# Sampled tokens' attention: eight PSUM banks dealt out as 3, 2 and 3 in place of 2, 2 and 4

## The reference: what is computed

```python
kc = compress(past_rows(pool_k_cmp), pos_k, w_k)      # 255 compressed keys per sequence
vc = compress(past_rows(pool_v_cmp), pos_v, w_v)
p_c = masked_softmax(einsum(qg, kc)); o_c = einsum(p_c, vc)
idx = top_k(block_score(p_c), 16)                     # 16 blocks of 64 tokens
o_s = softmax(q . k_slc over the chosen blocks) @ v_slc
o_w = softmax(q . 512-token window) @ v_win
o   = gate0 * o_c + gate1 * o_s + gate2 * o_w
```

## Time and profile before

| What | Value |
|---|---|
| median of 3 runs | 2275.66 us |
| the profiled execution, its own time | 2269.16 us |
| its span in the profile | 2267.4 us |
| the stage of the sampled tokens in that span | from about 1472 to 1734 us |
| a step of the first loop (8 of them) | 14.14 us |
| a step of the second loop (7 with keys to turn) | 12.98 us, two of them 1.4 us longer |
| TensorE busy over the span | 91% |
| DMA engines' busy share, first and second loop | 0.82 to 0.86, 0.81 to 0.98 |

### The profile page before, as it was taken

The page is one execution under the profiler, slowest core; times in us unless marked ns, Lnnn a source line. Parts: engine busy times, 40 slices in busy tenths (PEclk is TensorE's granted clock), DMA queues, the critical chain, the costliest instruction groups (busy, mean ns, idle before and its releaser), DMA issues. The chain is left out here.

```text
span 2267.4 us, 37830 instructions
## 1 busy us (share of the span) xinstructions
PE 2070.7 (91%) x16137; PEld 1393.5 (61%) x16137; DVE 868.8 (38%) x2212; ACT 581.1 (26%) x1481; POOL 132.4 (6%) x144
## 2 busy tenths in 40 slices
PE   8898989898989898599999999589878999999998
PEld 5565657575756565456777777455666666666543
DVE  3545364545454545301666666434321000010112
ACT  2323232323232223000445444233351000000000
POOL 1001010101000000000000000022120000000000
PEclk9999999999999999799999999799997999999999
DMA  4101010101020100402000000398695111110011
GB/s 134 38 11 49 11 49 12 48 11 48 14 54 19 41 21 2 148 19 68 20 10 11 11 10 1 92 321 298 246 348 173 42 33 32 32 48 17 0 65 60
DMA packets 121585, 151.22 MB, mean 67 GB/s; under 512 B 27866, under 2 KB 105090, under 8 KB 112866
## 3 DMA queue, kind: packets, MB, share of 16 engines
q1 hardware_dynamic: 110724, 76.78, 12.1%
q0 software_dynamic: 10704, 72.16, 8.9%
HBM read 136.83 MB, written 16.26 MB: 68 GB/s over the span
## 5 line engine op out<-in xcount | busy, mean ns | idle before, releaser
L824 PE MATMUL g_ps<-hT,W 128*128 128x352 f32 x1440 | 497.7, 474 | 0.2 <-issue 0.2
L824 PEld LDWEIGHTS g_ps<-hT,W 128*128 128x128 f32 x1440 | 253.4, 192 | 100.3 <-issue 7.5
L2550 DVE SCALAR_TENSOR_TENSOR m_sg<-m_sg,m_ps 128x352 f32<-128x352 f32 x48 | 25.0, 521 | 361.2 <-PE m_ps L2490 361.2
L1563 PE MATMUL p_ps<-hT,Wpair 128*128 128x352 f32 x384 | 129.4, 466 | 1.5 <-DMA Wpair<-in_w_in_dram 0.9
L2502 PE MATMUL m_ps<-m_Wo,m_mixed 128*128 128x512 f32 (+1 forms) x288 | 124.0, 592 | 1.4 <-DVE m_mixed L2553 1.4
L2516 ACT ACTIVATE m_sg<-m_ps 128x352 f32<-128x352 f32 x48 | 22.2, 463 | 387.6 <-PE m_ps L2483 387.6
L2483 PE MATMUL m_ps<-hT,Wgates 128*128 128x352 f32 x384 | 118.0, 466 | 1.5 <-DVEq L2539 1.5
L2483 PE MATMUL m_ps<-hT,m_Wgates 128*128 128x352 f32 x384 | 115.6, 459 | 0.0
L2483 PEld LDWEIGHTS m_ps<-hT,Wgates 128*128 128x128 f32 x384 | 74.1, 193 | 43.2 <-issue 1.9
L1979 PE MATMUL s_ps<-identity,s_G 128*128 128x128 f32 x512 | 75.6, 291 | 27.3 <-ACT s_XT L2194 19.3
L2483 PEld LDWEIGHTS m_ps<-hT,m_Wgates 128*128 128x128 f32 x384 | 73.0, 190 | 40.6
(11 more groups left out here) (416 smaller groups left out, 3366.9 us busy)
## 6 DMA issues: line engine op xcount, KB each, us to landing
W<-in_w_in_dram SPq DMA_DIRECT2D x32, 512.0 KB, 5.6
n_x<-in_x_prompt_dram SPq DMA_DIRECT2D x8, 512.0 KB, 7.8
g_S<-in_state_gdn_dram SPq DMA_DIRECT2D x8, 512.0 KB, 4.2
out_dram<-g_S POOLq DMA_DIRECT2D x8, 512.0 KB, 3.9
Wpair<-in_w_in_dram SPq DMA_DIRECT2D x16, 256.0 KB, 3.9
Wgates<-in_w_in_dram SPq DMA_DIRECT2D x8, 512.0 KB, 5.3
m_Wgates<-in_w_in_dram SPq DMA_DIRECT2D x8, 512.0 KB, 4.6
m_Wo<-in_w_out_dram SPq DMA_DIRECT2D x1, 4096.0 KB, 14.7
```

Of the source, the lines that this page charges most:

```text
L824: ins = pe.matmul(ps[:, k.bank, 0:w], W[:, c_, kt, :], hT[:, kt, t0:t0 + w], start=kt == 0, stop=kt == KT - 1)
L1563: ins = pe.matmul(ps[:, fill_bank(n), 0:w], W[:, "qz".index(x), kt, :], hT[:, kt, t0:t0 + w], start=kt == 0, stop=kt == KT - 1)
```

## The change

`RX` gets three banks in place of two, `RD` three in place of four, `RA` keeps two under other numbers. The start counts of the semaphores follow. Every engine has the same instructions in the same order as before; what changes is which bank a tile lies in and so what must have been emptied before TensorE fills it.

```diff
-        RX = Ring([0, 1], [x for n in range(SEQS) for x in keys(n)])
-        RA = Ring([2, 3], [f"{x}{i}" for i in range(NB) for x in ("S2", "sc")] + [f"T0{i}" for i in range(NB)])
-        RD = Ring([4, 5, 6, 7], ["blk", "gate", "lq"] + [f"{x}{i}" for i in range(NB) for x in ("pT", "V0", "V1")]
+        RX = Ring([0, 1, 2], [x for n in range(SEQS) for x in keys(n)])
+        RA = Ring([3, 4], [f"{x}{i}" for i in range(NB) for x in ("S2", "sc")] + [f"T0{i}" for i in range(NB)])
+        RD = Ring([5, 6, 7], ["blk", "gate", "lq"] + [f"{x}{i}" for i in range(NB) for x in ("pT", "V0", "V1")]
                   + ["imp", "ZT", "Oc0", "Oc1", "sel0", "sel1"]
                   + [f"{x}{i}" for i in range(NB) for x in ("s0", "s1", "w", "T1", "T2", "O")]
                   + ["nmT", "nmB", "sum", "tr"])
...
-            v.sem_inc(x_emptied, 2)
+            v.sem_inc(x_emptied, 3)
             v.sem_inc(a_emptied, 2)
-            v.sem_inc(d_emptied, 4)
+            v.sem_inc(d_emptied, 3)
```

## The result

The change takes 2256.73 us, the median of 7 runs (2251.05 to 2262.02), against 2275.66 for the kernel before (7 runs): a ratio of 0.9921, interval 0.9903 to 0.9939, so 14 to 22 us less. The forecast was 2263.7, the range 2258.5 to 2269.5: the sign is right, the gain is larger than I had allowed.

What follows compares the result with a forecast made beforehand. The prediction took TensorE's key transposes waiting for ScalarE's copies as the bound, with transfers close behind in the second loop. First loop 8.0 plus second loop 4.0 made 12.0 us: 2275.66 to 2263.7 us, range 2258.5 to 2269.5.

Steps and rivals of the forecast that it cites:

- The bound: Both loops: key transposes wait for ScalarE's copies, 46 times as matmuls, 40 as weight loads, 19.3 and 26.8 us.
- First loop, 8.0 us: First loop: 0.5 us saved in half 0, 1.0 us a step in all, eight steps, until VectorE's scaling is late.
- Second loop, as far as TensorE is concerned, 7.4 us: Second loop: values start at 7.37 for 8.41, 1.05 us a step over seven steps, before transfers are counted.
- Second loop: 4.0 us.: Second loop with transfers binding: 2.1 us of room, 0.5 from earlier key gathers, 1.4 of idle DMA time.
- The room of the gathers: Second loop: 2.1 us between a late value gather's landing and its matmuls, which a faster TensorE can eat up.
- The transfers bind at once: Rival, second loop: gathers issued earlier land no earlier, steps stay at 12.98 us, time 2267.7; chance 0.18.
- The transfers don't bind: Rival, second loop: the queue holds up to 417 GB/s, all of 8.0 + 7.4 comes, 2260.3; chance 0.18.
- Half the change does nothing: Rival: exponential waits for VectorE's maximum; only 0.5 us a first-loop step saved, nothing in the second, 2271.7; chance 0.07.
- Slower: Rival, both loops: gathers drawn together disturb each other, every step takes 14.46 us, +10.0, 2285.7; chance 0.03.
- VectorE's ring at nothing: VectorE's ring, four banks to three: no cost, since the window scores have 0.48 us of cover after O's copy.
- Clock, 1.7 us either way: Between the loops: the half-clock stretch may get longer or shorter by 1.7 us, put in the range only.
- The sum against the median: Whole kernel: 12.0 us subtracted from the median 2275.66, not the profiled 2269.16, which lies 6.5 us under it.

Runs made afterwards that it cites:

- The kernel with only this half: Three key banks as in the change, but from the second loop on each group waits as if there were two: 2260.87 us, 0.994 to before.

## Why the prediction was right in sign and too small in size

**The bound.** Right: in front of the third and fourth group stood the ring, and 39 of 46 waits are gone.

**First loop, 8.0 us.** Right in mechanism, measured 7.3: 0.91 a step for 1.0. VectorE's scaling is what is late next, and the third group waits for nothing. The kernel with only this half shows the same first loop, and those with the exponential moved show that the scaling was the bound: with it earlier, the step falls to 13.03 and 12.69.

**Second loop, as far as TensorE is concerned, 7.4 us.** Right: undisturbed steps take 11.90 to 11.92, where 11.93 followed from 1.05 us a step; 7 x 1.07 = 7.5.

**"Second loop: 4.0 us."** This step failed. It had two faults.
- *The room of the gathers was sized too small.* I let the transfers take 3.4 of 7.4. They took 2.0 in either profile: 86.1 and 85.4 against 7 x 11.91 = 83.4, less the 0.7 of the first profile's first step, which is the clock's. Behind the loop they took no more than before. The waits came as named: keys and values on gathers, late in the loop. Landings came later too, 9.9 us in the earlier trace rows, and for a gather of values issued between 1657 and 1658 of the change:

```profile
s_G<-in_cache_v_slc_dram,s_idx POOLq DMA_INDIRECT x1, 10.3
```

- *The stalls.* The two longer steps have no term in the sum. The prediction says only that the length of such a step "is not the transfers'", which is right, and so puts 3.2 us at nothing without a reason. The runs showed that they are the ends of code pieces that come late, at a place that belongs to the code, and whether the piece is late hangs on when TensorE gets there and when it was fetched. In the change the fetch for that place comes 7.3 us into its step (the window 1630.6 to 1630.9, the step from 1623.4), in before 11.0 us into it (1639.4, from 1628.4):

```profile
q8 instruction: 1, 0.02, 20.7%
```

  TensorE is there 3.6 us later (at 1634.23), more than the 2.2 to 2.7 from a fetch to the end of a stall. In the loop of before, away from the stalls, fetches begin 12.7 to 13.1 us apart, one a step, though four steps use five pieces; so each comes nearer to its use until one is late, and the extra one comes 6 to 7 us behind it. In the change some come 6 to 11 us apart without a stall. Why they come earlier there is not settled.

So the second loop gave 7.5 (TensorE) + 3.2 (stalls) - 2.0 (gathers) - 0.4 (clock in one first step, as a mean) = 8.3 us where the sum had 4.0. In all, the profiles give 7.3 (first loop) + 8.3 (second) - 1.2 (behind it) = 14.4 in place of 8.0 + 4.0. That alone would be 2261.3 us. The measured 18.0 [14 to 22] leaves some 3 to 4 us more, and where they come from is open: the stages of two profiles each (268.5 and 268.7 before, 256.3 and 250.0 after) differ by 15.5 in the mean, the whole spans (2267.4 and 2277.8; 2257.3 and 2253.9) by 17.0, and the two spans of before differ from each other by 10.4. The rest is of the size by which executions of one kernel differ outside the loops.

**The rivals.** "The transfers bind at once" fell: windows of the second loop draw 399 and 408 GB/s at a share of 1.01, and steps of 11.9 us come early in the loop. By the rule of the Trainium skill that it stood on (DMA: Bandwidth & Descriptors, Specifications, a limit of about 358 GB/s for a core) a step could not have become shorter; the trace does not bear that out. "The transfers don't bind" gave 2260.3, nearer to the measured time than the forecast, but by luck: they do bind late in the loop, and the stalls, which it does not name, pay for it. "Half the change does nothing" fell with steps of 13.23 and 11.9 us. "Slower" fell: no step of the change is over 13.01.

**VectorE's ring at nothing.** Right, and shown by itself: 0.9998 with three banks, 0.6 us a step lost with two.

**Clock, 1.7 us either way.** Right in size for the piece that it names: between the loops 26.0 and 23.4 us in two profiles of the same kernel. It also goes with the piece behind the loops (26.2 and 24.7).

**The sum against the median.** It was made against a profile that lay 6.5 us under its median. That did not hurt here, but a stage read from one execution is good to some 3 us at most: two profiles of the change differ by 6.3 in the stage.

## What to carry to other kernels

When a ring gets another bank, walk the chain of one step engine by engine and write down what is late next; that gave each step to within 0.1 us, and so did asking which tile reuses which bank when a ring gives one up. A queue at a share of 0.97 still had room for a tenth more traffic per time, so the share alone does not say that transfers bind; nor does the fastest rate of any window say that they don't, for by 417 GB/s they would have cost nothing and they cost 2.0 us. An idle stretch put down to "issue" on one engine, at one place in the code, may come from its instructions and not from its data: put it into the range, since any change of timing can make it vanish or come back.

## What I had not expected of the hardware

- TensorE stands still for 0.9 to 1.7 us when a piece of its code comes late. The stall comes round every four steps of the second loop, with five pieces of 16 KB fetched in between, and 128 transposes with their weight loads move the code by one whole piece. It does so at a DMA share of 0.64 as well as at 0.98.
- The gathers and loads of one core drew 408 GB/s over a window of 12.3 us, while the landings of values grew from 8.5 and 9.9 to 10.3 us.
